# A denoising layer with mixture of experts on one core: row buffers, the halves of one gate, and the layout of the gate and up weights

## The reference: what is computed

```
def ffn_sublayer(x, shift, scale, gate, g_pre_ffn, w_router, w_gate, w_up, w_down, g_post_ffn):
    h = modulate(x, g_pre_ffn, shift, scale)        # rms_norm(x, g) * (1 + scale) + shift
    return x + gate * rms_norm(expert_choice_moe(h, w_router, w_gate, w_up, w_down), g_post_ffn)

def expert_choice_moe(h, w_router, w_gate, w_up, w_down):
    cap = CAPACITY_FACTOR * T // N_EXPERTS          # 64 latent rows, 16 context rows per expert
    logits = jnp.einsum('btd,de->bte', h, w_router, preferred_element_type=jnp.float32)
    aff = jax.nn.softmax(logits, axis=-1)
    g, idx = lax.top_k(jnp.swapaxes(aff, 1, 2), cap)
    xg = jax.vmap(lambda hb, ib: hb[ib])(h, idx)
    a = jnp.einsum('becd,edf->becf', xg, w_gate)
    u = jnp.einsum('becd,edf->becf', xg, w_up)
    y = jnp.einsum('becf,efd->becd', jax.nn.silu(a) * u, w_down) * g[..., None].astype(h.dtype)
    return jax.vmap(lambda yb, ib: jnp.zeros((T, D), yb.dtype).at[ib.reshape(-1)].add(yb.reshape(-1, D)))(y, idx)
```

## Time and profile before

| what | value |
|---|---|
| median of 3 runs | 945.46 us (945.16 to 948.37) |
| the profiled execution, its own time | 947.62 us |
| its span, first to last instruction | 945.6 us |
| TensorE busy | 888.0 us, 94% of the span |
| VectorE, ScalarE, GpSimd busy | 365.0, 216.4, 102.6 us |
| moved by DMA | 269.31 MB, of it 251.42 MB on SyncE's queue |
| granted TensorE clock, mean | 0.982 of full |

### The profile page before, as it was taken

The page is one execution under the profiler, slowest core; times in us unless marked ns, Lnnn a source line. Parts: engine busy times, 40 slices in busy tenths (PEclk is TensorE's granted clock), DMA queues, the critical chain, the costliest instruction groups (busy, mean ns, idle before and its releaser), DMA issues. The chain is left out here.

```text
span 945.6 us, 19892 instructions
## 1 busy us (share of the span) xinstructions
PE 888.0 (94%) x8633; PEld 442.5 (47%) x8633; DVE 365.0 (39%) x974; ACT 216.4 (23%) x528; POOL 102.6 (11%) x137
## 2 busy tenths in 40 slices
PE   3999998899899999879999999999999999999985
PEld 3544444677655665533344443443443444433432
DVE  4256534887767765821112022021113120210136
ACT  3132213676645653410000000000000000000012
POOL 1021200000000000110110111011001101110225
PEclk9899999999999999889999999999999999999997
DMA  9997441400001119869999999999999999999984
GB/s 342 345 380 267 180 176 59 159 2 1 2 1 46 45 47 376 296 230 409 398 395 412 398 397 407 400 397 397 410 398 398 395 411 398 398 405 389 357 312 157
DMA packets 77717, 269.31 MB, mean 285 GB/s; under 512 B 6208, under 2 KB 9984, under 8 KB 77632
## 3 DMA queue, kind: packets, MB, share of 16 engines
q1 hardware_dynamic: 72384, 251.42, 68.0%
q0 software_dynamic: 4160, 13.90, 5.1%
q10 hardware_dynamic: 1088, 2.74, 0.7%
HBM read 252.06 MB, written 15.99 MB: 283 GB/s over the span
## 5 line engine op out<-in xcount | busy, mean ns | idle before, releaser
L954 PE MATMUL ps<-ring,reg 128*32 128x512 f32 x1792 | 201.6, 592 | 0.0
L1813 DVE TENSOR_SCALAR mod<-ps,kt 64x512 f32<-64x512 f32 x30 | 22.5, 749 | 254.8 <-PE ps L954 254.6
L954 PEld LDWEIGHTS ps<-ring,reg 128*32 128x32 f32 x1792 | 58.0, 110 | 113.3 <-issue 104.8
L968 PE MATMUL ps<-ring,values_in 128*32 128x256 f32 x1536 | 93.5, 386 | 2.2 <-ACT reg L1320 1.1
L1324 ACT ACTIVATE reg<-ps 128x256 f32<-128x256 f32 x16 | 6.1, 384 | 358.0 <-PE ps L1008 352.8
L954 PE MATMUL ps<-ring,kt 128*32 128x512 f32 x768 | 86.8, 592 | 0.0
L810 PE MATMUL ps<-ring,reg 128*128 128x512 f32 x160 | 76.4, 604 | 0.0
L968 PEld LDWEIGHTS ps<-ring,values_in 128*32 128x32 f32 x1536 | 50.2, 112 | 52.4 <-issue 23.9
L656 PE MATMUL ps<-ring,reg_qt 128*128 128x512 f32 x160 | 70.6, 594 | 0.0
L968 PE MATMUL ps<-ring,reg 128*32 128x256 f32 x1024 | 64.4, 395 | 1.8 <-DMA ring<-in_w_down 1.2
L1267 ACT ACTIVATE ring<-ps 128x640 f32<-128x640 f32 (+3 forms) x80 | 44.4, 555 | 72.1 <-PE ps L739 69.5
(11 more groups left out here) (238 smaller groups left out, 1000.0 us busy)
## 6 DMA issues: line engine op xcount, KB each, us to landing
ring<-in_w_up SPq DMA_DIRECT2D x32, 2048.0 KB, 21.3
ring<-in_w_down SPq DMA_DIRECT2D x32, 2048.0 KB, 21.2
ring<-in_w_gate SPq DMA_DIRECT2D x16, 2048.0 KB, 19.8
reg_qt<-in_w_gate SPq DMA_DIRECT2D x16, 2048.0 KB, 20.5
ring<-in_w_ada SPq DMA_DIRECT2D x12, 2048.0 KB, 12.6
reg<-in_x_sample SPq DMA_DIRECT2D x8, 512.0 KB, 6.3
ring<-in_w_in SPq DMA_DIRECT2D x2, 2048.0 KB, 14.0
ring<-in_w_out SPq DMA_DIRECT2D x2, 2048.0 KB, 10.1
```

Of the source, the lines that this page charges most:

```text
L954: last = pe.matmul(o[64 * n + r:64 * n + r + 32, :], x(4 * hf + j, r), w[:, j, n * HALF:(n + 1) * HALF], start=(hf == 0 and j == 0), stop= ...
L968: last = pe.matmul(o[32 * q:32 * q + 32, :], x(c), w[:, j, q * QUART:(q + 1) * QUART], start=(c == 0), stop=(c == KC - 1))
L1813: dve.tensor_scalar(put_l[:, n * HALF:(n + 1) * HALF], ps[rows, 3, :], g_l[rows, e:e + 1], None, ALU.mult)
```

## The change

- **Row buffers.** The output stage writes tile t to one of four buffers in turn, at columns 4096 to 8191 of `reg2_qt` (slot 7), in place of a tile each. The last tile shares the buffer of tile 0 and waits for its store.
- **Expert 1's gate.** Its first half is issued right after the reloads of x, once all projections are done. Its second half is issued behind the first gather of latent rows.
- **Runs of 16 KB.** A partition holds four neighbouring rows of each half of gate and up (row 512h + 4p + j). Features are then in another order, so the router rows, the pre gains and the modulation columns are loaded or turned in that order, and all transposes of x1 and of the gathered rows read every fourth element (`feature_block`). Down stays as it was.
- **Loads.** The router is loaded in two parts and the second set of pre gains in eight small loads; `columns` copies in halves of partitions and then multiplies.
- **Order.** `turn_lists` stands between the halves of up; VectorE forms the context activations after the copies of the lists; ten filling matmuls stand around `turn_aff(4)`.

The same replacement of `xn` by `rows_at` is left out where it repeats.

```diff
+        def feature_block(row, c):
+            return row.rearrange("p (h q j) -> p h j q", h=2, j=4)[:, c // 4, c % 4, :]
...
+        out_rows = reg2_qt[:, UNIT:2 * UNIT].rearrange("p (t d) -> p t d", t=4)
+        def rows_at(t):
+            return out_rows[:, t % 4, :]
...
-        N_CONSTS = 10
+        N_CONSTS = 19
...
-                sp.dma_start(wr[:, :].rearrange("p (c e) -> p c e", e=E),
-                             A["w_router"][0].rearrange("(c p) e -> p c e", p=P)).then_inc(consts_in, 16)
+                wr_rows = A["w_router"][0].rearrange("(h p j) e -> h p j e", h=2, j=4)
+                sp.dma_start(wr[:, 0:4 * E].rearrange("p (c e) -> p c e", e=E),
+                             wr_rows[0]).then_inc(consts_in, 16)
+                sp.dma_start(wr[:, 4 * E:].rearrange("p (c e) -> p c e", e=E), wr_rows[1]).then_inc(consts_in, 16)
+                ffn_columns = A["g_pre_columns"].rearrange("(q j) (m h b) -> b h m q j", j=4, m=2, h=2)
+                for b, h in itertools.product(range(4), range(2)):
+                    sp.dma_start(gpre[32 * b:32 * b + 32, KC + 4 * h:KC + 4 * h + 4], ffn_columns[b][h][1],
+                                 allow_slow_non_contiguous=True).then_inc(consts_in, 16)
...
-                src = w[0].rearrange("e (c p) n -> e p c n", p=P)[e][:, 4 * half:4 * half + 4, :]
-                sp.dma_start(ring_slot(s).rearrange("p (c n) -> p c n", c=4), src).then_inc(slot_in[s], 16)
+                if kind < 2:
+                    src = w[0].rearrange("e (h p j) n -> e h p (j n)", h=2, j=4)[e][half]
+                    sp.dma_start(ring_slot(s), src).then_inc(slot_in[s], 16)
+                else:
+                    src = w[0].rearrange("e (c p) n -> e p c n", p=P)[e][:, 4 * half:4 * half + 4, :]
+                    sp.dma_start(ring_slot(s).rearrange("p (c n) -> p c n", c=4), src).then_inc(slot_in[s], 16)
...
+            sp.wait_ge(proj_done, 3 * TILES)
+            expert_weight(1, 0, 0, SLOTS)
...
-            for half in (0, 1):
-                expert_weight(1, 0, half, SLOTS + half)
+            sp.wait_ge(gathered_l, 16)
+            expert_weight(1, 0, 1, SLOTS + 1)
...
-                for j in range(2):
-                    last = pe.transpose(ps[:, 7, j * P:(j + 1) * P], modq[:, m, j * P:(j + 1) * P], ident[:, :])
+                for j in range(4):
+                    last = pe.transpose(ps[0:P // 2, 7, j * P:(j + 1) * P], modq[:, m, j:QUART:4], ident[:, :])
...
-                                        xr[:, t, (4 * half + c) * P:(4 * half + c + 1) * P], ident[:, :])
+                                        feature_block(xr[:, t, :], 4 * half + c), ident[:, :])
...
-                    last = pe.transpose(ps[:, 5 + c // 4, c % 4 * P:(c % 4 + 1) * P], xg_c[:, c * P:(c + 1) * P], ident[:, :])
+                    last = pe.transpose(ps[:, 5 + c // 4, c % 4 * P:(c % 4 + 1) * P], feature_block(xg_c, c), ident[:, :])
-                    last = pe.transpose(ps[:, 5 + c // 4, c % 4 * P:(c % 4 + 1) * P], xg_l[:, c * P:(c + 1) * P], ident[:, :])
+                    last = pe.transpose(ps[:, 5 + c // 4, c % 4 * P:(c % 4 + 1) * P], feature_block(xg_l, c), ident[:, :])
...
                 if e == E - 2:
                     gate_l(e + 1, 1)
+            keep_busy(3, 6)
             turn_aff(4)
             pe.wait_ge(logits_ready, TILES)
+            keep_busy(3, 4)
             turn_rows_c(0)
             pe.wait_ge(gate_ready, 8)
             for half in (0, 1):
...
             pe.wait_ge(silu_done, 1)
             weight_in(2, 0)
             product_c(2, GC[:, QUART:], context_of(0))
+            turn_lists()
             weight_in(3, 0)
             product_c(3, GC[:, QUART:], context_of(0)).then_inc(up_c, 1)
-            turn_lists()
             turn_rows_c(1)
             pe.wait_ge(act_c_ready, 1)
             for j in range(2):
...
-            act.dma_start(gpre[:, :], A["g_pre_columns"]).then_inc(early_in, 16)
+            act.dma_start(gpre[:, 0:KC], A["g_pre_columns"][:, 0:KC]).then_inc(early_in, 16)
...
-                act.activation(xn[:, t, :].rearrange("p (a n) -> p a n", a=2), out_at(o), ACT.Square, scale=1.0 / 32.0,
+                act.activation(rows_at(t).rearrange("p (a n) -> p a n", a=2), out_at(o), ACT.Square, scale=1.0 / 32.0,
...
+                    act.wait_ge(rows_c_stored, 16)
...
-                    act.dma_start(rows_c, xn[:, 0, :]).then_inc(rows_c_stored, 16)
+                    act.dma_start(rows_c, rows_at(0)).then_inc(rows_c_stored, 16)
-                    act.dma_start(rows_l[(t - 1) * P:t * P], xn[:, t, :]).then_inc(rows_stored, 16)
+                    act.dma_start(rows_l[(t - 1) * P:t * P], rows_at(t)).then_inc(rows_stored, 16)
...
-            cols = ps[:, 7, 0:2 * P].rearrange("p (j q r) -> p q j r", j=2, q=4)
+            cols = ps[0:P // 2, 7, :].rearrange("p (j h u r) -> p u h j r", j=4, h=2, u=2)
-                    dst = cmod[:, n, cond, :].rearrange("p (q j) -> p q j", j=2)
-                    if n % 2 == 0:
-                        last = dve.tensor_copy(dst, cols[:, :, :, cond])
-                    else:
-                        g = gpre[:, (n // 2) * KC:(n // 2 + 1) * KC].rearrange("p (q j) -> p q j", j=2)
-                        last = dve.scalar_tensor_tensor(dst, cols[:, :, :, cond], 1.0, g, ALU.add, ALU.mult)
+                    for u in (0, 1):
+                        part = slice(P // 2 * u, P // 2 * (u + 1))
+                        last = dve.tensor_copy(cmod[part, n, cond, :].rearrange("p (h j) -> p h j", h=2), cols[:, u, :, :, cond])
+                if n % 2:
+                    dve.wait_ge(consts_in, 16 * N_CONSTS)
+                    link(last)
+                    for cond in (0, 1):
+                        g = gpre[:, (n // 2) * KC:(n // 2 + 1) * KC]
+                        last = dve.scalar_tensor_tensor(cmod[:, n, cond, :], cmod[:, n, cond, :], 1.0, g, ALU.add, ALU.mult)
...
-                dve.scalar_tensor_tensor(xn[:, t, :].rearrange("p (a n) -> p a n", a=2), out_at(o),
+                dve.scalar_tensor_tensor(rows_at(t).rearrange("p (a n) -> p a n", a=2), out_at(o),
...
-                dve.tensor_tensor(xr[:, t, :], xr[:, t, :], xn[:, t, :], ALU.add).then_inc(x1_ready, 1)
+                dve.tensor_tensor(xr[:, t, :], xr[:, t, :], rows_at(t), ALU.add).then_inc(x1_ready, 1)
...
                 half = slice(CAP_L * odd, CAP_L * (odd + 1))
                 last = dve.tensor_copy(get_l[half, :], ps[half, 0, odd:E:2])
             last.then_inc(rows_ready, 1)
-            dve.wait_ge(up_c, 1)
-            dve.tensor_tensor(a_c, s_c, ps[:, 2, QUART:], ALU.mult).then_inc(act_c_ready, 1)
             dve.tensor_copy(row_l[:, 0:E], ps[:, 0, 0:E]).then_inc(rows_ready, 1)
             dve.wait_ge(lists_turned, 2)
             dve.tensor_copy(g_l, ps[:, 1, 0:E]).then_inc(y_ready, 1)
+            dve.wait_ge(up_c, 1)
+            dve.tensor_tensor(a_c, s_c, ps[:, 2, QUART:], ALU.mult).then_inc(act_c_ready, 1)
             def modulate(pair):
```

More of the change, by code:

```diff
@@ L1215, in square_x1 @@
                 act.wait_ge(x1_ready, o + 1)
-                act.activation(xn[:, t, :], xr[:, t, :], ACT.Square, scale=1.0 / 32.0,
+                act.activation(rows_at(t), xr[:, t, :], ACT.Square, scale=1.0 / 32.0,
                                accum_out=ss2[:, t:t + 1]).then_inc(x1_squared, 1)
@@ L1225, in square_half @@
                     act.wait_ge(wout_done, TILES)
-                act.activation(xn[:, t, half * HALF:(half + 1) * HALF], out_at(o)[:, half, :], ACT.Square, scale=1.0 / 32.0,
+                act.activation(rows_at(t)[:, half * HALF:(half + 1) * HALF], out_at(o)[:, half, :], ACT.Square, scale=1.0 / 32.0,
                                accum_out=sso[:, t + half:t + half + 1]).then_inc(o_squared, 1)
@@ L1231, in square_x1_half @@
                 act.wait_ge(x1_ready, TILES + half)
-                act.activation(xn[:, t, half * HALF:(half + 1) * HALF], xr[:, t, half * HALF:(half + 1) * HALF], ACT.Square,
+                act.activation(rows_at(t)[:, half * HALF:(half + 1) * HALF], xr[:, t, half * HALF:(half + 1) * HALF], ACT.Square,
                                scale=1.0 / 32.0, accum_out=ss2[:, t + half:t + half + 1]).then_inc(x1_squared, 1)
@@ L1249, in normalise_x1 @@
                 act.wait_ge(x1_rstd, o + 1)
-                act.activation(xn[:, t, :], xr[:, t, :], ACT.Identity, scale=rs2[:, t:t + 1]).then_inc(xn_ready, 1)
+                act.activation(rows_at(t), xr[:, t, :], ACT.Identity, scale=rs2[:, t:t + 1]).then_inc(xn_ready, 1)
             def store_rows(o):
@@ L1623, in gate_half @@
                 dve.wait_ge(o_squared, o + 1 + half)
-                dve.tensor_tensor(xn[:, t, n], out_at(o)[:, half, :], gate_rows[:, 1, n], ALU.mult).then_inc(half_gated, 1)
+                dve.tensor_tensor(rows_at(t)[:, n], out_at(o)[:, half, :], gate_rows[:, 1, n], ALU.mult).then_inc(half_gated, 1)
             def add_half(half):
```

2 lines of the change are left out of this document (1 added, 1 removed).

## The result

The changed kernel takes **979.5 us** in the median of four runs (974.9 to 984.5), the kernel before 945.6 beside it: a ratio of 1.036, 95% interval [1.032, 1.040]. Forecast were 937.8, range 934 to 945. The time is far outside, and on the side to which the prediction gave 0.10.

What follows compares the result with a forecast made beforehand. TensorE was taken to bound the experts, with the weight stream close behind. The terms -7.1 (entry), -0.7 (16 KB runs) and +0.1 (column transposes) sum to -7.7 us, taking the median 945.46 to 937.8; range 934 to 945.

Steps and rivals of the forecast that it cites:

- Runs of 16 KB for gate and up: Experts' weight loads: longer runs save part of the 1.24 us weight wait; -0.7 us taken, bounds -1.2 and +0.8.
- what is late next: Entry to the experts: ScalarE's emptying of context rows, ending 409.7, frees TensorE, not the gather at 408.3; 4.5 us sooner.
- Lists turned between the halves, gate 1 in halves: Entry to the experts: gather issued 1.7 us sooner, landing with free queues; latent product 7.1 us earlier, 4.5 waiting, 2.6 clock.
- rival B: Entry: clock at 1.2 GHz behind the gather all the same; gain at the latent product 4.5 us, total 940.4; chance 0.13.
- move nothing by themselves: Entry: filling matmuls go where TensorE idles, 390 to 392 us, and change nothing, since the lists come from VectorE.
- The gather's landing there: Entry: with no weights beside it the latent gather lands in 4.2 us, at worst 8.4.
- rival D: Entry: gather not helped by free queues, landing after 8.4 us; TensorE gains 1.8 us, total 943.1; chance 0.07.
- 16 KB runs at the weights: Experts: -0.7 us from less waiting for weights; the stream's reserve melts about 1 us per expert and is gone by 864.
- Transposes: Attention and experts: reading every fourth element costs nothing, bounds nothing to 0.9 us per eight; modulation's column transposes +0.1 us.
- Rival A: Slow strided transposes: 0.45 us for each of 14 groups, 6.3 us, total 943.5; chance 0.22.
- The start: Before attention: nine small loads issue the three ada loads 8 us later, within 10 us of slack; cost 0, worst 1 us.
- Rival C: Experts: 16 KB runs read more slowly, the weight stream becomes the bound; 5% slower costs 15 us, total 953; chance 0.10.

Runs made afterwards that it cites:

- e8: The changed kernel with each latent gather issued one expert earlier and twelve more filling matmuls before the lists are turned: 939.1 us, ratio 0.993.
- e5: The kernel before with only the latent gathers issued one expert earlier: 945.0 us, ratio 1.000.
- e9: The kernel before with only the transposes of x1, context rows and latent rows reading every fourth element: 945.7 us, ratio 1.001.
- e2: The changed kernel, 16 KB runs kept, with each latent gather issued one expert earlier: 941.2 us, ratio 0.995.
- e10: The changed kernel without the new feature layout (4 KB runs), with gathers one expert earlier and twelve more filling matmuls: 943.1 us, ratio 0.997.
- e7: The changed kernel with each half of gate and up loaded by two transfers in 8 KB runs: 944.1 us, ratio 0.998.
- e11: The changed kernel with each half of gate and up loaded as two transfers of 64 partitions, runs still 16 KB: 1276.7 us, ratio 1.340.
- e3: The kernel before with only the gate and up loads changed to 16 KB runs: 980.7 us, ratio 1.036.
- e12: The kernel before with gate and up read in 8 KB runs, one load for each half: 948.6 us, ratio 1.003.

## Why the prediction was wrong, step by step

**The step that failed** is *Runs of 16 KB for gate and up*. It priced the longer runs by what they do to the weights, and by nothing else. The parts go by "what is late next" only in the entry. Of the eight gathers the two there were read (8.4 and 4.2 us), and the six of the steady state weren't: what they do was put at nothing without a reason. Their rows were in the trace: issue 8.3 us before use, landing 7.7, one already late by 0.51 us. The step's bounds, -1.2 and +0.8 us, left out every other user of the queues. Measured: -1.5 us at the weights, +41.7 at the gathers. The final line of the prediction named what would show it ("the experts no longer follow in 32.8 and 31.9 us"), but no rival stood behind it.

**The rule of the queue.** Row first: the share of GpSimd's own queue hardly moves, 5.1% of 945.6 us before and 5.0% of 981.1 after, for the same 4160 packets:

```profile
q0 software_dynamic: 4160, 13.90, 5.0%
```

So GpSimd's packets don't last longer; the gather is longer under way, so they wait more. That they wait for their turn behind weight packets is argued from this and from the run's length, and no row shows a single turn. The Trainium skill, DMA: Bandwidth & Descriptors, Queues, rings and completion order, says that each engine goes round the queues that have work and takes a whole packet from one before it changes to the next. An estimate from rows: at 405 GB/s over 16 engines a run of 4 KB takes 0.16 us, one of 16 KB 0.65. A gather of 128 rows has eight per engine; with one weight run, taken as one packet, ahead of each it would add 1.3, 2.6 and 5.2 us to the 4.2 of empty queues, giving 5.5, 6.8 and 9.4 for 4, 8 and 16 KB. Measured, with the gather in its old place, are 7.9 to 8.0, 8.5 to 9.0 and 12.8 to 13.4 (issued one expert earlier: 8.4 to 8.8, 9.5 and 12.2). The direction agrees, the size doesn't: little from 4 to 8 KB, 1.6 to 1.7 times from 4 to 16. The estimate also lets down, whose runs stay at 4 KB, go by. What makes the difference stays open.

**Lists turned between the halves, gate 1 in halves.** Right in kind. The gather went out 1.03 us behind the lists' turning and landed in 4.3 us. TensorE then waited for ScalarE and not for the gather, as forecast:

```profile
399.77 1.93 PE L990 MATMUL ps<-ring,values_in 128*32 128x256 f32 x32 [0.49 <-ACT reg L1341]
404.40 0.43 PE L938 MATMUL ps<-ident,kt 16*128 16x16 f32 x2 [2.69 <-DVE kt L1792]
404.76 3.56 PE L990 MATMUL ps<-ring,values_in 128*32 128x256 f32 x32
...
410.27 1.93 PE L990 MATMUL ps<-ring,reg 128*32 128x256 f32 x32 [0.56 <-ACT reg L1349]
412.97 1.23 PE L955 MATMUL ps<-ident,reg 128*128 128x128 f32 x8 [0.77 <-ACT values_in L1335]
414.13 1.93 PE L990 MATMUL ps<-ring,reg 128*32 128x256 f32 x32
415.88 4.47 PE L976 MATMUL ps<-ring,reg 128*32 128x512 f32 x40
```

The size is 5.0 us, not 7.1. The prediction let the first half of up be done just when the lists are. With the filling matmuls the clock stays high, the half is done at 401.7, and TensorE idles 2.69 us for the lists. Then the clock falls, and the second half takes 3.56 us where 1.83 were put down; ScalarE's context rows, which stand behind it, come 1.7 us later because of it. That is rival B's cause in another place: ahead of the gather, not behind it, and at two thirds of its price of 2.6. The filling matmuls, which "move nothing by themselves", moved this. e8 shows it: with twelve more the entry is 1.6 us shorter than in the changed kernel, and the term becomes 28.5 - 21.8 = 6.7 us, nearly the 7.1. That nearness is in part luck, since the 28.5 is of a long execution. There gate's context product, 64 records at 395.04, took 5.60 us, with the clock at 0.5 from 392.5 on the earlier trace rows; in e5, the same program up to here, it took 4.88:

```profile
392.30 4.88 PE L968 MATMUL ps<-ring,values_in 128*32 128x256 f32 x64 [0.64 <-ACT values_in L1310]
```

The prediction read its terms off the long execution and then took off the 2.16 us between it and the median, as if none of these lay in its terms. Between this execution and that of e5, 1.7 us lie in the entry, so part of the gain was counted twice. Against e5 and e9 the term is 3.1 to 3.4 us in the changed kernel and 4.7 to 5.0 in e8.

**The gather's landing there,** forecast at 4.2 us, was 4.3: rival D is out.

**16 KB runs at the weights.** -0.7 forecast, -1.5 measured (33.36 to 31.90 us for the expert that waited, in e2 as well, where no other wait helps the stream). And the reserve: the prediction said that the stream has none left. With 4 KB that is so (e10: 3.4 us of waits); with 8 KB or more it has.

**Transposes.** Nothing forecast; +0.08 us per eight at 2.4 GHz, 0.6 us in the whole kernel with an interval that holds zero. Rival A, 6.3 us, is out. The Trainium skill, Advanced Engine Details and Errata, SBUF Cachelines, as the prediction cites it, agrees in direction only: a weight load of the strided operand takes 211 in place of 141 ns, and most of that is hidden behind the matmuls.

**The start.** Forecast 0, at worst 1 us, and 0.1 for the column transposes. It cost more. The three ada loads go out 5.0 us later (51.38 for 46.36; the prediction put 8), but the second of them takes 19.4 us to land where the prediction went on with 13.1, and TensorE waits for it:

```profile
68.06 1.93 PE L604 MATMUL ps<-ring,reg 128*32 128x256 f32 x32
71.24 1.93 PE L604 MATMUL ps<-ring,reg 128*32 128x256 f32 x32 [1.25 <-DMA ring<-in_w_ada]
```

No kernel without the nine small loads waits at this product; of the seven with them three do (1.2, and 0.5 in e7 and e11). The one descriptor per element that the prediction gives the gains' loads is borne out: packets under 512 B go from 6208 to 6608, which is 1024 more for the gains, 768 fewer for the router's longer rows and 16 for each of the nine loads. The column transposes take 0.44 us more, not 0.1. From the start of this ada product to the start of the last one it is 70.2 us in all seven kernels without the new loads, 72.1 in the changed kernel and 70.6 to 71.4 in the other six. So this part costs 0.4 us, and up to 1.9. The wait at the first ada product is another matter, 1.0 us after and 2.2 before:

```profile
PE ps L561 <- DMA ring<-in_w_ada: 2.2, 1, 2.2
```

It lies between 0.9 and 2.3 us in kernels of both kinds. The product began at 42.71 in this execution of the kernel before, at 40.05 in the changed one, and at 40.4 to 40.5 in e3, e5, e9 and e12. The +1.4 of the books is thus -2.7 up to the first ada product, +1.9 from the second to the last, and +2.2 in the rest of attention. That rest differs by up to 1.7 us between kernels whose attention is that of the kernel before, so how much of it the change makes stays open.

**Rival C** had the right sign and the wrong mechanism. The runs aren't read more slowly, and no wait for an expert's weight appears. Its 953 came from a stream that falls behind, which did not happen, and lies 26 us below what was measured.

**Without the gathers' waits** the sum stands close: e2, which differs from the changed kernel in the gathers' order alone, took 941.2 us. That is inside the range and 3.4 above the forecast. Of this at least 2.1 are the entry, 0.6 the strided and 0.3 the column transposes, less 0.8 at the weights; the rest is within the spread of its runs (938.3 to 942.2).

## What to carry to other kernels

Before making one stream's transfers longer or denser, list everyone else who uses the same queues in the steady state, and subtract each one's issue-to-landing time from its issue-to-use time. A difference near nothing (here 8.3 - 7.7 us) is the first thing that the edit will break, and each long miss costs the wait and then the clock. Issue such small transfers as early as their buffer allows; here it cost nothing that shows (e5), and it is what made the longer runs pay. And before a term is read off one execution, see how long the same stretch takes in another: here the entry of the same program took 26.8 and 28.5 us.

## What the runs showed that was not expected

- The time of a gather of 512 KB beside a stream of weights depends on the stream's run length, with the larger step between 8 and 16 KB: 7.9 to 8.0, 8.5 to 9.0 and 12.8 to 13.4 us in the median, 4.2 with empty queues. GpSimd's two scatters go the same way, from 7.8 and 6.9 us before to 9.6 and 9.5 in the changed kernel.
- With 4 KB runs in gate and up the stream gives 401 GB/s and falls behind; with 8 and 16 KB it keeps up at the 408 and 412 that TensorE takes. These few GB/s decide whether TensorE waits.
- Loads over 64 partitions, two for each half, ran at 241 GB/s in the experts against some 400, with the queues as busy: 1.34 times the whole time.
- Behind full work in the experts an idle time of 1.48 us left the eight transposes at 1.21 us, the speed of the higher clock; those of 5.08 us and more were each followed by 3.4 to 6.2 us of work at 1.2 GHz, and that of 2.69 us in the entry by 3.6.
